# Attention units whose first transposes of head 0 stand in their own turn on TensorE

## What is computed

```python
for blk in range(seqlen // Q_BLOCK):          # 8 query blocks of 128
    q0 = blk * Q_BLOCK
    kend = q0 + Q_BLOCK
    s = (q_nope @ k_nope[:kend] + q_rope @ k_rope[:kend]) * scale
    p = softmax(where(mask, s, -inf))
    outs.append(p @ v[:kend])
```

## Time and profile before

| | |
|---|---|
| median of three runs | 3405.72 us (3404.87 to 3407.22) |
| profiled execution | 3401.22 us, its span 3399.6 us |
| granted TensorE clock, mean | 0.984 of full speed |
| TensorE busy | 3215.0 us, 95% of the span |
| VectorE, ScalarE, GpSimd busy | 61%, 38%, 11% |
| first attention | 244.7 to 453.6 us |
| second attention | 2309 to 2460 us |

### The profile page before, as it was taken

How to read it: one execution, slowest core, us unless ns; L and a number is a source line. 1 busy time by engine, 2 the same in 40 slices (tenths; PEclk the granted TensorE clock), 3 DMA queues, 4 the chain that set the end, 5 groups by cost and what they waited for, 6 DMA issues and landing times.

```text
span 3399.6 us, 39667 instructions
## 1 busy us (share of the span) xinstructions
PE 3215.0 (95%) x15804; PEld 2529.8 (74%) x15804; DVE 2066.8 (61%) x2774; ACT 1293.3 (38%) x1907; POOL 376.1 (11%) x405
## 2 busy tenths in 40 slices
PE   8998899999999998899999999998879899999998
PEld 6765576878777786578888877785567778888877
DVE  5545566664555646777776556675564777766334
ACT  2564434442525344643233224313434443223123
POOL 1000000110302011100000003140011300000012
PEclk9999999999999999899999999999989999999999
DMA  6210111222423122332224243322153332224232
GB/s 155 49 41 5 54 50 52 72 87 75 100 50 106 50 88 74 101 110 82 80 76 164 95 143 102 110 64 84 17 107 130 108 121 87 75 99 166 80 113 99
DMA packets 363254, 299.39 MB, mean 88 GB/s; under 512 B 55104, under 2 KB 324896, under 8 KB 362784
## 3 DMA queue, kind: packets, MB, share of 16 engines
q1 hardware_dynamic: 340800, 215.17, 22.0%
q0 software_dynamic: 22272, 81.69, 7.3%
HBM read 240.32 MB, written 52.95 MB: 86 GB/s over the span
## 4 chain that ended last, share of the span: by engine, by line
PE 74%; DVE 12%; ACT 6%; DMA 5%; issue 3%; SPq 1%; POOL 0%; ACTq 0%; DVEq 0%; POOLq 0%
PE PS L364 41%; PE PS L2450 12%; PE PA L2450 7%; DMA CDX<-ssd_decays 3%; PE PS L864 2%; PE PA L875 1%; DVE WL L328 1%; DVE CDX L1999 1%; PE PB L1778 1%; DVE XL L2127 1%; PE PB L887 1%; ACT PP L975 1%; DMA WS<-in_ffn_w_out_dram 1%; PE PA L404 1%; PE PB L1781 1%
## 5 line engine op out<-in xcount | busy, mean ns | idle before, releaser
L364 PE MATMUL PS<-XH,WH 128*128 128x512 f32 x1744 | 603.6, 405 | 37.9 <-DVE XL L2127 20.2
L364 PE MATMUL PS<-XL,WH 128*128 128x512 f32 x1744 | 580.3, 392 | 0.0
L364 PE MATMUL PS<-XH,WL 128*128 128x512 f32 x1744 | 579.4, 391 | 0.0
L321 ACT ACTIVATE WH<-WS 128x1024 fp32r<-128x1024 f32 (+1 forms) x243 | 240.3, 992 | 843.4 <-PE PS L364 793.0
L364 PEld LDWEIGHTS PS<-XH,WH 128*128 128x128 f32 x1744 | 326.5, 189 | 137.0 <-DVE XL L2127 27.9
L364 PEld LDWEIGHTS PS<-XH,WL 128*128 128x128 f32 x1744 | 329.2, 189 | 70.3
L364 PEld LDWEIGHTS PS<-XL,WH 128*128 128x128 f32 x1744 | 329.1, 189 | 69.4 <-issue 2.0
L328 DVE TENSOR_TENSOR WL<-WS,WH 128x1024 fp32r<-128x1024 f32 (+1 forms) x243 | 284.8, 1172 | 142.8 <-ACT WH L321 142.5
L364 PE MATMUL PS<-TQH,WH 128*128 128x512 f32 x448 | 161.5, 395 | 7.0 <-DVE WL L328 7.0
L364 PE MATMUL PS<-TQL,WH 128*128 128x512 f32 x448 | 160.2, 392 | 0.0
L364 PE MATMUL PS<-TQH,WL 128*128 128x512 f32 x448 | 160.1, 392 | 0.0
(11 more groups left out here) (683 smaller groups left out, 6167.2 us busy)
## 6 DMA issues: line engine op xcount, KB each, us to landing
RAW<-in_ffn_w_in_dram SPq DMA_DIRECT2D x36, 1024.0 KB, 5.3
WS<-in_ffn_w_out_dram SPq DMA_DIRECT2D x48, 512.0 KB, 3.5
WS<-in_ssd_w_in_dram SPq DMA_DIRECT2D x40, 512.0 KB, 3.7
DEC<-ssd_decay_sums SPq DMA_DIRECT2D x32, 512.0 KB, 4.1
WS<-in_ffn_w_in_dram SPq DMA_DIRECT2D x32, 512.0 KB, 3.8
CDX<-ssd_decays SPq DMA_DIRECT2D x56, 256.0 KB, 4.8
TQF<-ffn_hidden POOLq DMA_DIRECT2D x14, 1024.0 KB, 8.3
x_residual<-ACC POOLq DMA_DIRECT2D x6, 2048.0 KB, 8.0
```

The costliest lines, as they stand in the source:

```text
L321: nc.scalar.activation(WH[:, s, 0:cols], WS[:, s, 0:cols], ACT.Copy).then_inc(W_HI[s], 1)
L364: last = nc.tensor.matmul(PS[s][0:width, c], w[:, s, k * width:(k + 1) * width], x[:, k, c], start=(k == 0 and j == 0), stop=(k == kt - 1 ...
```

## The change

For units from block 4 on, head 0's first four transposes (`turn(pe, v, 0, 0)`) are issued in the step of their own unit, after `weigh` of the unit two before and ahead of head 1's second group of the unit before. Before, they were issued one step later, behind the scores of the next unit. Head 0's second group now comes first behind the scores, and head 1's first group after it. For blocks 0 to 3 nothing changes. No other engine's program is changed.

```diff
                 t = v - 1 if v0 < v <= v1 else None
                 if t is not None:
-                    self.turn(pe, t, 0, 0)
+                    self.turn(pe, t, 0, t % TT >= 4)
                     self.turn(pe, t, 1, 0)
-                    if t % TT >= 4:
-                        self.turn(pe, t, 0, 1)
                 if v >= v0 + 2:
                     self.weigh(pe, v - 2)
+                if v < v1 and v % TT >= 4:
+                    self.turn(pe, v, 0, 0)
                 if t is not None and t % TT >= 4:
                     self.turn(pe, t, 1, 1)
```

## The result

The changed kernel takes 3386.24 us (median of 5 runs, 3385.95 to 3390.32) against 3404.87 us of the kernel before (5 runs, 3401.81 to 3407.22) on the same chip: ratio 0.995, 95% interval 0.9939 to 0.9961, so 17.0 us faster (13.3 to 20.8). The forecast was 12.8 us, 3392.9, with a range down to 3388.0: the sign was right, the size too small, and the time lies outside the range, by 1.8 us. (Executions far above the others of their kernel are left out of every comparison; there was one, 9647 us, among twelve of the variant that changes the first attention alone.) The profiled execution took 3386.24 us (span 3384.6), 15.0 less than the one profiled before.

A forecast was written before the change was run, and what follows sets the result against it. TensorE's products mostly bound the kernel; inside the attentions, waits through old copies on ScalarE. Gains of 5.6 us (first attention) and 7.2 (second), together 12.8, took 3405.72 to 3392.9 us; range 3388.0 to 3400.5.

The forecast's parts named there:

- The chain through the old copies: Blocks 5 to 7: old transposes and copy delay new exponentials; gains 0.66, 0.72, 0.79 us per step in the second attention.
- Rival (d): Exponentials overlapped with VectorE's pass lengthen by what they start earlier, so no net gain; about 3405.7 us; chance 0.09.
- Step 4: From block 4's scores to the next: 0.27 waiting plus 0.58 work, 0.85 us lost per pair, except second attention's first.
- Rival (b): Block 4's step costs nothing, its delay absorbed by block 4's exponentials: 5.95 us more gained, 3387.0; chance 0.08.
- Step 0: First block of the next pair: 0.63 us gained each time in the second attention, 0.83 in the first.
- The last step of the first attention: Block 7 of the last pair: no scores follow and the second group waits for its copy instead; gain 0.
- Step 5 of the first attention: Block 5, pairs 0 to 2: bound by VectorE's rotation, the maxima and head 1's copy; 0.11 us lost each.
- step 6: Block 6's scores to the next: 1.28 us gained in first attention's pairs 0 to 2, 0.53 in its last; second 0.72.
- no clock to win back: TensorE's granted clock read as 1.00 (2.4 GHz) in a steady head pair, so no gain from the clock was expected.

The follow-up runs named there:

- the variant with long waits: Block 4 to 7's own-turn transposes moved one place earlier than in the changed kernel, ahead of `weigh`: ratio 1.0074 (1.0059 to 1.0089), 25 us slower than the kernel before.

## Why the prediction was right, and where it was wrong

**The chain through the old copies** (steps 5, 6, 7): right to 0.1 us. For the gain of the three steps, 0.66, 0.72 and 0.79 were forecast for the second attention, 0.57 to 0.66, 0.72 and 0.78 measured; first attention 1.28 and 0.64 forecast, 1.33 and 0.64 measured. The limit that I named, VectorE's maximum of head 1, is the new one. Rival (d), longer exponentials, falls by their rows.

**Step 4**: 0.85 forecast, 0.87 and 0.88 measured, 0.68 in the first attention's first pair; nothing in the first pair of the second attention, as said. Putting the group behind the spread and the projection showed that in the first attention's pairs with a projection the delay of these is the cause (all of the loss went away), and that in the second attention it is 0.29 of wait and 0.58 of work. Rival (b), the loss absorbed, falls. The group of four took 0.58 behind its wait (2384.68 to 2385.26), as in the rows. By the figure of the Trainium skill (TensorE: Matmul & The Clock Gate, Part 4: PE-mode transpose) for a single transpose, some 275 ns and measured on bf16, step 4 would have lost an estimated 1.37, which no pair at full clock shows. As the duration of one the figure fits, though these are float32 (median 273 ns in the trace of before); as the price of one in a row it doesn't, because the four overlap.

**The terms that were mis-sized**, all too low. Step 0: I let head 0's second group wait "for a copy of 0.60 that begins as the scores do". The copy begins at 2367.13, 0.15 ahead of the scores: it starts 0.10 before the exponential's short read-out record is over, and the scores 0.05 after that. It is done at 2367.72, the scores at 2367.77, so the group goes without a wait, and unwaited it is cheap: the gain is 0.83 and 0.84 instead of 0.63 (0.6 us over three pairs), and 0.90 to 0.91 instead of 0.83 in the first attention (0.2). The last step of the first attention: 0.2 instead of 0. Step 5 of the first attention: 0 instead of 0.11 lost in three pairs (0.3): the last transpose of head 1 follows the moved four without its own start. The smaller ones, step 6 and the first pair's step 4 above all, come to 0.2. In all 1.5 us, which makes 14.3 of 12.8. A term that the prediction didn't have at all: in the last step of the second attention the first product behind it (L897) comes 13.43 after the last scores instead of 13.78, another 0.3.

**The step that failed**: "no clock to win back". I had read a granted clock of 1.00 from one trace whose steady pairs happened to be free of half-clock stretches. That was chance: of the four traces of that kernel it is the only one that has none from step 4 of the first pair on in either attention. (Nor does the 1.00 tell whether transposes count as busy, as the prediction took it: only 72 of that pair's 281 records are transposes.) Over the traces of the unchanged two kernels and of the two variants with one attention changed, the attentions with the old order (the four of the kernel before, and for each attention the variant that left it alone) and those with the new one (the three of the changed kernel and the other variant) were this long, from the first scores to the first product behind the attention (us):

| | old order, five traces | new order, four traces | difference of means | steps |
|---|---|---|---|---|
| first | 208.9, 215.4, 215.4, 208.9, 208.9 | 205.1, 202.5, 203.2, 202.7 | 8.1 | 6.6 |
| second | 156.3, 158.7, 159.3, 159.3, 158.7 | 149.3, 149.0, 149.6, 149.6 | 9.1 | 7.7 |

The sum, 17.2 us, is near what the three comparisons say (17.0, 19.4, 16.3). The steps explain 14.3, the product behind the second attention another 0.3, and the remaining 2.6 go with half-clock stretches.

In the second attention, 1.1: step 4 of pair 2 took 5.7 to 5.8 instead of 4.20 in four of five old traces, and 5.07 or 5.08 in all new ones. Since the variants with block 5 old in the first attention have the changed second attention too, that is none of seven traces. In the first, 1.5: the stretches in steps 6 and 7 (3.4 us in two of five old traces, none in four new ones) make 1.35 of it. Those in pair 0 (3.3 us in step 4 of two old traces, 3.0 in one new) and the new order's own in step 4 of pairs 1 and 2 (1.0 and 1.4 us in two of four new traces, none in the old) nearly cancel.

So that the clock gave something back is counted, in the first attention over few traces; why it did is not shown. For shorter idle times as the cause speaks the variant with long waits, whose clock fell much more. Against it: the variant with only step 6 old did not reproduce the pattern; the same gap of 1.9 stood ahead of a full clock and of a half one; and the stretch in step 4 of pair 2 of the second attention stands behind gaps of 0.33 and 0.90 that the new order has at the same places with the clock at full. What decides in which place and in which execution a stretch falls stays open.

**The range** was cut too close: half of rival (b) was left out below, and nothing had been allowed for the clock. A bound at (b)'s own 3387.0, lower by the clock's 2.6 us, would have held the time. That the gain is larger than 12.8 is not chance, for the steps alone have 14.3. That the time fell outside the range is partly chance: 3405.72 less the 17.2 us found above is 3388.5, just inside. The kernel before had a median of 3404.87 in this comparison, 0.85 lower, and the other 1.4 us are scatter between executions; the changed kernel's medians in the three comparisons were 3386.24, 3382.91 and 3388.26, of which the last lies inside. Without the clock's 2.6 us the steps and the 0.3 would have left 3391.1.

## What to carry to other kernels

When an engine works through units in a strict queue, look for old work standing between a unit's input and its output, and move it into the wait of the unit before; the gain is the distance to the next limit, which can be read off as the time between that limit's release and the actual start. Put the moved work behind everything that others wait for: the same four transposes cost 0.9 us ahead of a projection and nothing behind it. Where no projection follows, what remains is their own work, 0.5 to 0.6. Compare step lengths, which repeat to 0.02 us, rather than totals, which differ by 10 us and more between executions; and look at the granted clock in more than one trace before taking it as given.

The version with block 4's group behind the projection is the best by its steps, 3.8 us shorter than the changed kernel; the totals don't tell the two apart.

## What the runs showed of the hardware

A copy on ScalarE starts some 0.10 us before the read-out record of the exponential ahead of it ends (2367.13 against 2367.04 + 0.19). TensorE's granted clock fell to half, 1.2 GHz, inside a stage in which it was busy 86% of the time (186.22 of 215.37 us), and at places that are the same from trace to trace but not in every trace: the first attention of one and the same kernel was 208.9 us or 215.4 us long.
